# Attention's input products in three fp32r passes, tables and fills moved between engines, a third buffer in one projection, and a halved last copy

## What is computed

```python
def recurrent_block(...):            # its last product is y*hr @ w_out
    return (y * hr) @ w_out
def shared_kv(h, kv_norm, kv_w, ...):
    u = rmsnorm(h, kv_norm)
    kv = (u @ kv_w).reshape(B, S, 6, N_KV_GROUPS, HEAD_DIM)
    k_c, v_c, k_s, v_s, k_w, v_w = [kv[:, :, j] for j in range(6)]
    k_s = rope(rmsnorm(k_s, k_norm[1]), pos)
    k_w = rope(rmsnorm(k_w, k_norm[2]), pos)
    k_cmp = compress(k_c, ...)       # v_cmp = compress(v_c, ...)
def nsa_layer(h, norm_g, w_in, ...):
    z = rmsnorm(h, norm_g) @ w_in
    q = rope(rmsnorm(z[..., :1024], q_norm_g), pos)
    gates = sigmoid(z[..., 1024:] + gate_b)      # 48 columns
```

## Time and profile before

| what | value |
|---|---|
| median of 3 runs | 2324.26 us (2321.26 to 2324.26) |
| the profiled execution's own time | 2323.76 us |
| its span, first to last instruction | 2322.2 us |
| granted TensorE clock, mean | 0.998 |

### The profile page before, as it was taken

How to read it: one execution, slowest core, us unless ns; L and a number is a source line. 1 busy time by engine, 2 the same in 40 slices (tenths; PEclk the granted TensorE clock), 3 DMA queues, 4 the chain that set the end, 5 groups by cost and what they waited for, 6 DMA issues and landing times.

```text
span 2322.2 us, 30322 instructions
## 1 busy us (share of the span) xinstructions
PE 2293.6 (99%) x11616; PEld 1902.5 (82%) x11616; DVE 1694.8 (73%) x1617; ACT 1378.1 (59%) x1249; POOL 104.5 (5%) x111
## 2 busy tenths in 40 slices
PE   8999999999999999999999999999999999999998
PEld 7988857988888878888987788888888888888886
DVE  7755545754557776645667788888888888889897
ACT  4643314653356855433568566777777777777775
POOL 0000020000001200000011010000000000000020
PEclk9999999999999999999999999999999999999999
DMA  7555445165625346445343499999999999999993
GB/s 242 182 200 216 145 141 184 62 237 198 217 84 181 109 145 253 176 162 205 118 152 120 147 357 415 417 405 370 388 368 387 369 391 366 392 367 391 367 387 125
DMA packets 205668, 588.55 MB, mean 253 GB/s; under 512 B 9180, under 2 KB 19616, under 8 KB 205584
## 3 DMA queue, kind: packets, MB, share of 16 engines
q1 hardware_dynamic: 198736, 564.28, 65.0%
q0 software_dynamic: 6656, 23.04, 2.6%
q10 hardware_dynamic: 192, 0.05, 0.0%
HBM read 573.19 MB, written 14.16 MB: 253 GB/s over the span
## 4 chain that ended last, share of the span: by engine, by line
PE 96%; DVE 2%; ACT 1%; issue 0%; DMA 0%; DVEq 0%; ACTq 0%
PE ps L1471 9%; PE ps L1470 9%; PE ps L1472 9%; PE ps L811 8%; PE ps L813 8%; PE ps L812 8%; PE ps L1510 4%; PE ps L1509 4%; PE ps L1511 4%; PE ps L689 3%; PE ps L1239 2%; PE ps L1241 2%; PE ps L1240 2%; PE ps L681 2%; PE ps L1173 1%; PE ps L699 1%
## 5 line engine op out<-in xcount | busy, mean ns | idle before, releaser
L2172 DVE TENSOR_TENSOR more_low<-more_parts,high_parts 128x2048 fp32r<-128x2048 f32 x192 | 432.0, 2288 | 33.6 <-ACT high_parts L1578 32.5
L1578 ACT ACTIVATE high_parts<-more_parts 128x2048 fp32r<-128x2048 f32 x192 | 364.6, 1918 | 101.2 <-PE ps L1511 51.8
L1470 PE MATMUL ps<-high_parts,xmh 128*128 128x512 f32 x896 | 352.3, 393 | 0.0
L1472 PE MATMUL ps<-high_parts,xml 128*128 128x512 f32 x896 | 349.1, 390 | 0.0
L2172 DVE TENSOR_TENSOR raw_low<-raw,high_parts 128x2048 fp32r<-128x2048 f32 x144 | 324.0, 2287 | 26.6 <-ACT high_parts L1578 26.6
L1578 ACT ACTIVATE high_parts<-raw 128x2048 fp32r<-128x2048 f32 x144 | 276.0, 1921 | 92.0 <-PE ps L1472 47.5
L1725 ACT ACTIVATE wh<-raw 128x4096 fp32r<-128x4096 f32 (+1 forms) x55 | 189.5, 3446 | 188.1 <-PE ps L813 177.4
L2349 DVE TENSOR_TENSOR wl<-raw,wh 128x4096 fp32r<-128x4096 f32 (+1 forms) x55 | 230.4, 4190 | 70.2 <-ACT wh L1725 70.2
L811 PE MATMUL ps<-wh,xh 128*128 128x512 f32 (+1 forms) x632 | 243.8, 386 | 1.8 <-issue 1.2
L813 PE MATMUL ps<-wh,xl 128*128 128x512 f32 (+1 forms) x632 | 239.6, 379 | 0.0
L812 PE MATMUL ps<-wl,xh 128*128 128x512 f32 (+1 forms) x632 | 239.5, 379 | 0.0
(11 more groups left out here) (555 smaller groups left out, 4327.1 us busy)
## 6 DMA issues: line engine op xcount, KB each, us to landing
more_parts<-in_moe_w_gate SPq DMA_DIRECT2D x78, 1024.0 KB, 5.1
more_parts<-in_moe_w_up SPq DMA_DIRECT2D x66, 1024.0 KB, 7.0
raw<-in_moe_w_down SPq DMA_DIRECT2D x64, 1024.0 KB, 6.8
more_parts<-in_moe_w_down SPq DMA_DIRECT2D x48, 1024.0 KB, 6.1
raw<-in_moe_w_up SPq DMA_DIRECT2D x46, 1024.0 KB, 5.2
raw<-in_w_in SPq DMA_DIRECT2D x22, 2048.0 KB, 8.0
raw<-in_f_w_in SPq DMA_DIRECT2D x20, 2048.0 KB, 8.5
raw<-in_moe_w_gate SPq DMA_DIRECT2D x34, 1024.0 KB, 6.9
```

Of the source, the lines that this page charges most:

```text
L1470: mm(o, xmh[:, k, :], hi[:, cs], start=(k == 0), stop=False)
L1472: t = mm(o, xml[:, k, :], hi[:, cs], start=False, stop=(k == KD - 1))
L1578: fn(part_high(j), part_raw(j), ACT.Copy).then_inc(hi_done, 1)
L2172: v.tensor_tensor(part_low(j), part_raw(j), part_high(j).bitcast(F32), ALU.subtract).then_inc(lo_done, 1)
```

## The change

1. Recurrent projection: quarter 2 has a buffer of its own (`wm3`), and its high and low copies are made before the first columns are transposed. In `ffn0`'s first block the gated product `hidden` goes ahead of the low part of the down weights on DVE.
2. Attention inputs: all five wide tiles and the gate columns are split. ACT makes a high part of each half tile, DVE a low part. Tokens get high and low parts `uh`, `ul`, `ubh`, `ubl`. The gate columns are loaded once by POOL at the start, so a slot tile falls away.
3. The rotation tables move from DVE to POOL, the zero fill from POOL to ACT, the copies of keys and values to ACT, and the two late key phases of 128x256 become one of 128x512. The compressed scores' maxima and weights move into the attention loop.
4. At the end ACT copies both halves, the first as soon as bank 3 is done, and the rows are given back by halves.

```diff
         def out_high(site, q):
-            return wm3 if site > 1 and q == 2 else wmo[:, q % 2]
+            return wm3 if site != 1 and q == 2 else wmo[:, q % 2]
...
+        ENTRY_HIGH = {("kv", 0): (0, 1), ("b_in", 0): (0, 1), ("b_in", 1): (2, 0), ("kv", 1): (1, 2), ("kv", 2): (0, 3)}
+        ENTRY_AFTER = {("b_in", 0, 0): ("kv", 0, 0), ("b_in", 0, 1): ("kv", 0, 1), ("b_in", 1, 1): ("b_in", 0, 0),
...
+            def entry_product(key, hi_, lo_, tokens=None, between=None, rings=(me.v, me.a)):
+                banks = []
+                for half in range(2):
+                    me.see(mh_ready)
+                    me.see(ml_ready)
+                    hi, lo = entry_high(key, half), entry_view(key, half, raw_low)
+                    for m, ring in enumerate(rings):
+                        if half == 0:
+                            if tokens:
+                                turned(tokens[m])
+                            banks.append(ring.claim(pe))
+                        o, ms = ps[:, banks[m], :], slice(m * P, (m + 1) * P)
+                        for kk_ in range(4):
+                            k = 4 * half + kk_
+                            mm(o, hi_[:, k, ms], hi[:, kk_, :], start=(k == 0), stop=False)
+                            mm(o, hi_[:, k, ms], lo[:, kk_, :], start=False, stop=False)
+                            t = mm(o, lo_[:, k, ms], hi[:, kk_, :], start=False, stop=(k == KD - 1))
...
-            turned(0)
-            keys_values(0)
-            turned(1)
-            product(me.a, ("kv", 0), 1, uT)
...
+            entry_product(("kv", 0), uh, ul, tokens=(1, 2))
+            entry_product(("b_in", 0), ubh, ubl, tokens=(3, 4))
+            entry_product(("b_in", 1), ubh, ubl)
...
+            entry_product(("kv", 1), uh, ul, between=hidden_products, rings=(me.a, me.a))
...
+            window_part(me.a, 0, 0)
+            window_part(me.a, 1, 0)
...
+            window_part(me.a, 0, 1)
+            turn_keys(0)
+            window_part(me.a, 1, 1)
+            released(("kv", 2), me.a)
+            turn_keys(1)
...
+            def high_entry(key, half):
+                arrived(act, key)
+                if (*key, half) in ENTRY_AFTER:
+                    act.wait_ge(*entry_used[ENTRY_AFTER[(*key, half)]])
+                elif key == ("kv", 0):
+                    act.wait_ge(u_done, FFN_END["ffn0"])
+                fn(entry_high(key, half), entry_view(key, half), ACT.Copy).then_inc(mh_ready, 1)
...
+            def low_entry(key, half):
+                me.see(mh_ready)
+                v.tensor_tensor(entry_view(key, half, raw_low), entry_view(key, half), entry_high(key, half).bitcast(F32),
+                                ALU.subtract).then_inc(ml_ready, 1)
...
                     if site == 0:
                         low_gate_half(name, 1, B0 + 1, 1)
-                    low(name, 2, B0, w0 // P * D)
+                    if site:
+                        low(name, 2, B0, w0 // P * D)
                     hidden(U0, w0, small[:, 6:7])
+                    if site == 0:
+                        low(name, 2, B0, w0 // P * D)
                     low_h(U0, w0)
...
-        COMPRESSED_AT = [1, 2]
+        COMPRESSED_AT = [3, 4]
...
             maxima(1)
-            me.see(cexp_ready)
-            link(v.tensor_reduce(cstat[:], cs[:], AX.X, ALU.add))
...
+            compressed_scores()
             for i in range(1, len(STEPS)):
                 if i + 1 < len(STEPS):
                     maxima(i + 1)
                 outputs(i - 1)
+                if i == 1:
+                    compressed_weights()
...
+                            if last and c == 3 and half == 0:
+                                t.then_inc(d_half, 1)
...
+                    act.wait_ge(d_half, len(FFN) + 1)
+                    fn(last_rows[:, 0:FB], ps[:, 3, :], ACT.Copy).then_inc(ye_half, 1)
                     act.wait_ge(used, part_count(29, it))
                     fn(last_rows[:, FB:], ps[:, 4, :], ACT.Copy).then_inc(ye_half, 1)
...
-                    take_rows(last_rows, 29, it, (0,))
```

More of the change, by code:

```diff
@@ L215, in weight_plan @@
     tile("kv", 0)
-    for t in range(3):
+    for t in range(2):
         tile("b_in", t)
@@ L936, in _, with turned @@
             ffn("ffn0", (me.e, me.f))
[L939 to L945, removed]
+            def turned(n):
+                for s_ in (e_read, f_read):
+                    pe.wait_ge(s_, n)
+            rows_made = [0]
+            def entry_product(key, hi_, lo_, tokens=None, between=None, rings=(me.v, me.a)):
[15 more added lines that the diff above has]
+                            t = mm(o, lo_[:, k, ms], hi[:, kk_, :], start=False, stop=(k == KD - 1))
+                        if half:
+                            t.then_inc(ring.filled, 1)
+                        elif m:
+                            t.then_inc(rows_used, 1)
+                            rows_made[0] += 1
+                        if between and half and m == 0:
+                            between()
+                    entry_used[(*key, half)] = (me.a.filled, me.a.n) if half else (rows_used, rows_made[0])
+                released(key, me.a)
             def turn_keys(w):
@@ L1036, in window_part @@
                 t.then_inc(ring.filled, 1)
-            arrived(pe, ("kv", 2))
-            window_part(me.v, 0, 0)
+            for half in range(2):
+                me.see(mh_ready)
+                me.see(ml_ready)
+            window_part(me.a, 0, 0)
+            window_part(me.a, 1, 0)
             me.see(kc_ready)
@@ L1844, in _ @@
             marks["kvc_a"] = me.a.n
-            root(NH // 2)
+            high_entry(("b_in", 0), 1)
+            high_entry(("b_in", 1), 0)
+            high_entry(("b_in", 1), 1)
+            act.wait_ge(small_in, GATES_IN)
+            fn(gates_high[:], gates_raw[:], ACT.Copy).then_inc(mh_ready, 1)
             queries(0)
             root(NH // 2)
+            fn(zeroed[:], C("one")[:, 0:1].to_broadcast([P, zeroed.shape[1]]), ACT.Copy, scale=0.0).then_inc(zeroed_set, 1)
             root(NH // 2)
@@ L1850, in _ @@
             root(NH // 2)
-            me.see(gate_ready)
+            root(NH // 2)
+            act.wait_ge(q_ready, M)
             fn(gate[:], gate[:], ACT.Sigmoid).then_inc(gated, 1)
-            b = me.a.take(act)
-            fn(hidden_n, ps[0:NG * NCMP, b, :], ACT.Copy).then_inc(a_read, 1)
+            high_entry(("kv", 1), 0)
+            high_entry(("kv", 1), 1)
+            for kv in range(2):
+                b = me.a.take(act)
+                fn(hidden_n[:, kv * CH:(kv + 1) * CH], ps[0:NG * NCMP, b, 0:CH], ACT.Copy).then_inc(a_read, 1)
             for m in range(M):
@@ L2974, in _, with take_rows @@
             t.then_inc(ye_taken, 1)
-            def take_rows(dst, j_down, it, halves=(0, 1)):
+            def take_rows(dst, j_down, it):
                 dve.wait_ge(used, part_count(j_down, it))
-                for half in halves:
+                for half in range(2):
                     t = v.tensor_copy(dst[:, half * FB:(half + 1) * FB], ps[:, 3 + half, :])
@@ L3104, in _ @@
             dve.wait_ge(rows_added, 2)
-            for m in range(M):
-                for half in range(2):
+            for half in range(2):
+                for m in range(M):
                     me.see(put_done)
```

376 lines of the change are left out of this document (223 added, 153 removed).

## The result

The changed kernel takes 2328.55 us (median of 11 runs, 2321.80 to 2331.65) against 2324.26 of the kernel before (11 runs beside them, 2321.26 to 2326.57). The ratio is 1.0018 with a 95% interval of 1.0010 to 1.0026: slower by 4.3 us, where 11 less were forecast. The profiled execution took 2330.06, its span is 2328.5, 6.3 more than before, and its mean granted clock is 0.992 (0.998 before).

A forecast was written before the change was run, and what follows sets the result against it. PE, busy 99% of the span, was taken as the bound. -1.4 - 9.1 + 0.3 - 0.9 = -11.1 from a span of 2322.2, plus 1.56 around it, gave 2312.7, as a median 2313.1 (range 2310.5 to 2315.5).

The forecast's parts named there:

- Part 1: Recurrent projection: the third quarter's own buffer closes a PE wait, -1.4 us; the swap at ffn0's start counts as nothing.
- Part 2: PE's list in the attention inputs: split products save time, gate columns lose 1.3, net -12.9 us; wide matmuls step at 0.2275.
- Part 3, up to the second query tile: Attention inputs: PE waits 0.7 and 0.15 before the first query half; query tile 1 ends near 324.2.
- the DRAM round trip, done near 319, is off the path: Attention inputs, part 3: the round trip ends near 319, before PE needs it, so it costs nothing.
- Clock: Narrow gate products and compression: same clock loss as before, about 1.1 us; bounds -1.1 and +1.4.
- The late waits: Late keys, part 3: PE waits 0.3 at the keys, 2.1 at the fourth window part, 0.4 at second key transposes.
- Part 4: Moved small work: DVE does about 2 us more in the attention loop's first three steps, +0.3; bounds 0 and +1.
- Part 5: The end: halved last copies let PE start the rows back earlier; 0.9 us survives, bounds -0.7 and -1.4.
- (b): Attention inputs: DVE falls behind, perhaps through POOL's table products (priced about 3), +3 to +6, 2316 to 2319; chance 0.22.
- (a): Attention inputs: no waits and the `hb` swap pays, 3.8 + 0.6 on top, 2308.7; chance 0.12.
- (c): Passes are saved but waits of 7 to 15 give nearly all back, 2319.6 to 2329; chance 0.08.
- (d): Attention inputs: high parts wait for the half just used, copy, subtraction and products in series, 30 on top, 2343; chance 0.08.

The follow-up runs named there:

- ends_only: The kernel before with only the projection's third buffer, the gated part first and the halved last copies; attention inputs as before: 2320.74 us, ratio 0.9988.
- pause: late_fill with ten useless GpSimd fills ahead of the compressed input's DRAM round trip, so PE waits about 5 us: 2330.89 us, ratio 1.0025.
- late_fill: The changed kernel, with SP filling the first compression tile only when the compressed input is back from DRAM: 2318.11 us, ratio 0.9980.
- filler: The changed kernel with 22 useless 512-column products where PE waits for the compressed input: 2325.54 us, ratio 1.0008.
- gates_both: late_load with the gate products in two pieces, the first between wide products of the second query tile: 2315.19 us, ratio 0.9967.
- late_load: late_fill with the gate columns loaded by GpSimd two down products before ffn0's end instead of at the program's start: 2318.59 us, ratio 0.9979.
- gates_apart: late_fill with the 48 gate products in two pieces of 24, the first between wide products of the second query tile: 2316.86 us, ratio 0.9972.

## Why the prediction was wrong

DVE worked 73.4 us in the stage (284.36 to 395.94) for the forecast's 76; the error is not in what the engines had to do.

- **Part 1, -1.4: right.** From the first input products to ffn0's first down products the changed kernel gains 1.6 (+0.73 to -0.87), ends_only 1.58. Over the twelve profiled executions with this part it is 1.0 to 2.0, but for pause, which gains nothing there, and no run says why. The waits of the earlier trace rows are gone, and `hl` is late as forecast (0.6 expected):

```profile
113.14 0.47 PE L844 MATMUL ps<-wh,hh 128*128 128x512 f32 x1 [0.73 <-DVE hl L2490]
```

- **Part 2, the wide products: right, a little short.** 48 of them go from 301.78 to 312.97, 0.233 each instead of 0.2275, which over 192 is 1.1 us. It is also slower than the 0.23 that the prediction named as a sign against it; the sign came true, at this small price. The narrow ones step at 0.111 while the clock is high (325.70 to 328.26 for 23 steps in late_fill), as forecast.
- **Part 3, up to the second query tile: right within 0.6.** The list has PE done near 324.2, 7.3 before 331.54, and it leaves out the 1.4 of part 1: 8.7 in all. Measured from the first input products PE is done 8.1 earlier (-7.41 less +0.73). That 324.13 stands so close to the 324.2 of the list is luck: the one includes part 1 and a start 0.73 late, the other neither. The wait before the first query half is 0.90 for 0.7 + 0.15.
- **Part 3, "the DRAM round trip, done near 319, is off the path": this step failed.** I took its 3 and 2.4 us from the kernel before and moved only its start. The change's own list says that a slot tile falls away, but I did not write SP's list anew without it: its issues behind that tile were the one list that I had not laid beside the others. Two fills of 2 MB moved up by 17 and 19 us, onto the trip. Its write took 8.5 us and its last reads up to 8.8, where they had been 3.1 and 2.4. PE's wait by itself cost 5.1 us, and the low clock that came with it 5.7.
- **Clock, "I take the same loss; bounds -1.1 and +1.4": this term was mis-sized.** From the trace of before only 3.4 us at half clock were to be seen ahead of an unbroken PE. The split gate products turned 4.1 us of narrow work into 5.4 and the stretch at half clock into 6.8 even without a wait (late_fill, filler), and a second one came right behind the late wait. The wait alone does not bring it: gates_both and late_load have the same wait, 1.75 and 1.76 us, and no low stretch there. Counting half of each low stretch as lost, an estimate, that is (6.8 + 3.4 - 3.4) / 2 = 3.4 us more. It is rather less, since not every low stretch costs half: the 3.4 us from 377.3 cost 1.1 (8.93 us from the fourth window part to the first scores, against 7.88 in gates_both, where the clock is high), and 6.8 us at the start of the loop cost 1.7 (21.71 in gates_apart against 20.05). With the round trip's wait the low stretches were 20.5 and 6.8.
- **The late waits: right.** 1.76 and 0.28 against 2.1 and 0.4; the 0.3 at the first key transposes did not come.
- **Part 4, +0.3 for the loop: low.** From the first scores to the later step it takes 18.72 before and 20.05 in late_fill, where the clock is not low in between: +1.3, above the upper bound of 1.
- **Part 5, -0.9: right.** From the later scores to the rows given back the offset falls by 1.25 (+7.08 to +5.83); 0.47 of it is lost again by the end of the span, which leaves 0.78. Counted only from the start of the last down product to the end of the span, 12.88 us before, it is 0.6 to 0.8 in all twelve profiled executions with this part (12.11 to 12.32 us): a little below the forecast, and in some below its bound of 0.7.
- **The sum, where it can be checked.** late_fill is the kernel that I had in mind. Its span is 2317.07 against 2322.15, -5.1 for the forecast's -11.1. Of the 6.0 between them some 3 are clock (the 3.4 above at most), 1.0 loop, 1.1 wide steps, and 0.4 start; what is left is within the spread of the parts.
- **Rivals.** (b) held for the size of one hand-off only (below). (a) did not happen. (c), with a chance of 0.08, forecast this time range and waits of 7 to 15; PE's waits in the stage are 0.48, 0.90, 5.11, 1.76 and 0.28, 8.5 in all. But (c) named no cause, and it gave nothing for the clock, which took as much as the one large wait. (d) did not happen: no high part waited for the half just used. My list of what would prove me wrong, "PE waits of over 10 us in this stage", did not come true though the prediction failed, and it shows the same gap: I looked for the loss in ACT and DVE, never in the DMA engines.

## What to carry over

When a load is dropped from a round of slots, every later load moves up: write the issue times of that queue anew, and lay each large one beside the small transfers that someone waits for. A short transfer on the path is held back by a large one that nobody needs yet, and holding the large one with one wait was worth 9 to 10 us here. Where PE stands still, the price is more than the wait: 5.3 and 5.7 us of it cost 11 and 14. Narrow products can be dealt out between wide ones; for the gates of 48 columns that was worth about 3 us in one pair of kernels, and 1 in another, which is not clear of noise (for the transposes it was not tried). And a gain made by closing small waits may be taken back by the clock.

## What the runs showed of the hardware

TensorE's clock can fall without any wait. In late_fill PE was busy 5.81 of 5.90 us with transposes of 120 and products of 48 columns at 2.4 GHz, and then had 1.2 GHz for 6.8; with 24 of the 48 between wide ones, three of four profiled executions kept 2.4, and one had 1.2 for 3.4 us. Useless products in a wait made the program faster.

One GpSimd product and one DVE subtraction take longer side by side than alone. In the changed kernel the GpSimd rows are

```profile
292.53 0.32 POOL L3463 TENSOR_TENSOR rope_k<-const,bc 128x64 f32<-128x64 f32 x1
292.81 2.36 POOL L3462 TENSOR_TENSOR rope_k<-const,bc 128x64 f32<-128x64 f32 x1
295.14 0.31 POOL L3463 TENSOR_TENSOR rope_k<-const,bc 128x64 f32<-128x64 f32 x1
```

and the DVE rows beside them and after them

```profile
292.04 2.96 DVE L2579 TENSOR_TENSOR raw_low<-raw,wmh 128x2048 fp32r<-128x2048 f32 x1
...
299.39 2.29 DVE L2579 TENSOR_TENSOR raw_low<-raw,wmh 128x2048 fp32r<-128x2048 f32 x1 [2.05 <-ACT wmh L1883]
```

The subtraction takes 0.67 longer than its like, and one product of GpSimd takes 2.36 instead of 0.32 and ends where the subtraction ends. This is rival (b) at work, at 0.7 us and not at 3: it stands in the chain before the first query half, where PE's wait was 0.90. All eleven profiled executions with split inputs have the same pair, 2.36 beside 2.94 to 2.97. "SBUF — State Buffer" of the Trainium skill, in "SBUF: two separate sides", says that a VectorE instruction with two SBUF inputs and a GpSimd instruction that reads SBUF do not share their ports: whichever starts first holds them for its whole length, and the other is blocked. The rows agree in that the long product ends with the subtraction. But the two products before it, at 292.25 and 292.53, kept their 0.32 although the subtraction's row had begun at 292.04. That fits if the subtraction itself waited until about 292.7, which would be its extra 0.67; no row shows it.
